# Row sums of w_ada: ScalarE multiplies, GpSimd adds one piece per slab, VectorE takes the last 20 pieces

## What is computed

```python
c_act = jax.nn.silu(c)
mod = c_act @ w_ada[l] + b_ada[l]                  # w_ada: 2048 x 12288
sh1, sc1, gt1, sh2, sc2, gt2 = jnp.split(mod, 6, axis=-1)
h = modulate(rms_norm(x, g_mix[l]), sh1, sc1)
z = h @ w_in[l]                                    # q, k, v of two attentions, index, two gates
# stick-breaking attention, indexed sparse attention, their output products, merge
x = x + gt1[:, None, :] * (merged @ w_out[l])
h = modulate(rms_norm(x, g_ffn[l]), sh2, sc2)
a = causal_dwconv(h @ w_gate[l], conv_w[l], conv_b[l])
y = (jax.nn.silu(a) * (h @ w_up[l])) @ w_down[l]
x = x + gt2[:, None, :] * y
```

## Time and profile before

| | |
|---|---|
| median of 3 runs | 3091.49 us (3090.83 to 3091.84) |
| span of the profiled execution | 3088.4 us |
| PE busy | 2772.0 us (90%) |
| DVE busy | 2006.4 us (65%) |
| ACT busy | 1288.5 us (42%) |
| POOL busy | 1037.5 us (34%) |
| mean granted clock of PE | 0.960 |

### The profile page before, as it was taken

One profiled execution on the slowest core, in us unless ns is written; L12 is line 12 of the kernel. 1 busy time (PEld: TensorE's weight loads), 2 busy tenths in 40 slices (PEclk: granted clock), 3 DMA queues, 4 the chain that ended last, 5 costly groups with the idle time before them and its releaser, 6 DMA issues. The chain is left out here.

```text
span 3088.4 us, 35464 instructions
## 1 busy us (share of the span) xinstructions
PE 2772.0 (90%) x12279; PEld 2258.1 (73%) x12279; DVE 2006.4 (65%) x1808; ACT 1288.5 (42%) x1505; POOL 1037.5 (34%) x538
## 2 busy tenths in 40 slices
PE   0599899989988799999999959998898999999998
PEld 0477787667767678888788748777587888888886
DVE  7776566887975777677766674456655555555554
ACT  1223455334433444444444434444245444444443
POOL 0598454858945433222322250002200111111111
PEclk9989899989999899999999979998999999999999
DMA  9666554746664665655666515454054555555553
GB/s 392 240 205 230 198 206 175 245 144 210 242 234 164 236 204 190 204 195 191 198 204 207 187 55 187 153 177 150 1 164 152 190 190 190 190 191 190 189 190 122
DMA packets 266919, 585.40 MB, mean 190 GB/s; under 512 B 14300, under 2 KB 16676, under 8 KB 263900
## 3 DMA queue, kind: packets, MB, share of 16 engines
q1 hardware_dynamic: 266844, 584.41, 56.1%
HBM read 582.26 MB, written 2.11 MB: 189 GB/s over the span
## 5 line engine op out<-in xcount | busy, mean ns | idle before, releaser
L1206 DVE TENSOR_TENSOR sb_wlo<-sb_raw,sb_whi 128x1024 fp32r<-128x1024 f32 x896 | 1322.9, 1487 | 883.4 <-ACT sb_whi L818 882.5
L818 ACT ACTIVATE sb_whi<-sb_raw 128x1024 fp32r<-128x1024 f32 x896 | 945.2, 1059 | 1452.8 <-PE lin L393 1250.8
L391 PE MATMUL lin<-sb_whi,sb_act_hi 128*128 128x512 f32 x2880 | 1154.9, 401 | 89.7 <-DVE sb_wlo L1206 46.4
L393 PE MATMUL lin<-sb_whi,sb_act_lo 128*128 128x512 f32 x2880 | 1136.2, 395 | 0.0
L392 PE MATMUL lin<-sb_wlo,sb_act_hi 128*128 128x512 f32 x2880 | 1136.0, 394 | 0.0
L391 PEld LDWEIGHTS lin<-sb_whi,sb_act_hi 128*128 128x128 f32 x2880 | 550.7, 191 | 218.9 <-issue 53.2
L393 PEld LDWEIGHTS lin<-sb_whi,sb_act_lo 128*128 128x128 f32 x2880 | 549.6, 191 | 117.9
L392 PEld LDWEIGHTS lin<-sb_wlo,sb_act_hi 128*128 128x128 f32 x2880 | 551.3, 191 | 111.8 <-issue 0.2
L1758 POOL TENSOR_TENSOR sb_ada_in<-sb_ada_in,sb_small 128x1024 f32<-128x1024 f32 x128 | 301.0, 2351 | 293.5 <-DMA sb_ada_in<-in_w_ada_dram 174.7
L1760 POOL TENSOR_TENSOR sb_ada_acc<-sb_ada_acc,sb_ada_in 128x1024 f32<-128x1024 f32 x128 | 383.4, 2995 | 10.0
L391 PE MATMUL lin<-sb_whi,sb_hid_hi 128*128 128x512 f32 x704 | 278.4, 395 | 6.3 <-DVE sb_hid_lo L1487 3.7
(11 more groups left out here) (292 smaller groups left out, 1770.5 us busy)
## 6 DMA issues: line engine op xcount, KB each, us to landing
sb_raw<-in_w_in_dram SPq DMA_DIRECT2D x88, 1024.0 KB, 5.9
sb_raw<-in_ffn_w_gu_dram SPq DMA_DIRECT2D x88, 1024.0 KB, 5.1
sb_ada_in<-in_w_ada_dram SPq DMA_DIRECT2D x128, 512.0 KB, 3.9
sb_raw<-in_gla_w_in_dram SPq DMA_DIRECT2D x48, 1024.0 KB, 5.2
...
```

Of the source, the lines that this page charges most:

```text
L391: pe.matmul(o, x_hi[:, kt + q, t], whi[:, w], start=first and q == 0, stop=False)
L393: m = pe.matmul(o, x_lo[:, kt + q, t], whi[:, w], start=False, stop=last and q == 1)
L818: act.activation(whi[:, idx % RING * HALF:(idx % RING + 1) * HALF], raw[:, idx // 2 % RING, idx % 2 * HALF:(idx % 2 + 1) * HALF], ACT.Copy ...
L1206: dve.tensor_tensor(wlo[:, c], raw[:, idx // 2 % RING, idx % 2 * HALF:(idx % 2 + 1) * HALF], whi[:, c].bitcast(fp32), ALU.subtract).then_i ...
```

## The change

1. **Multiply on ACT, add on POOL.** For chunks 0 to 107 ACT multiplies in place (`ada_scale`), right after it has split the second half of the slab the chunk belongs to. POOL only adds (`ada_add`), and copies instead of adding for the first row block of a piece, so `ada_acc` is no longer cleared. The column copy (`acol`) is gone.
2. **One table places the chunks.** `CHUNKS_AT` gives to each slab, counted from the first of A, its chunks: none for the first four slabs, then one a slab through A, B and to the 12th slab of C1 (chunks 0 to 63), one a slab through C2 and O (64 to 95), four in U's last four slabs, and eight in F1p (one each in slabs 0, 1, 4 and 5, two each in slabs 6 and 7). SP issues the chunk behind its slab; it waits for the addition two chunks earlier (`ada_done`).
3. **The last 20 chunks (108 to 127), two in each round of F1, go to DVE** as one fused multiply and add (`ada_last`), behind the splits of halves 21 and 23.
4. **Moved steps.** `ada_columns(0)` stands after B (on a buffer of its own, `ada_first`), `ada_columns(1)` inside C1 after half 11 of its second round; `gs_ffn` is made after B; the 16 small loads and the wait for `erow`'s write stand behind the first slab of the second round of C1.
5. **Loops A, B, C1, C2, O** are unrolled on SP, ACT and DVE, C1 on PE too. POOL's stages of the attentions keep their order among themselves.

```diff
+ADA_PIECES = (4, 3, 2, 5)
+CHUNKS_AT = {}
+for _n in range(108):
+    _at = 4 + _n if _n < 64 else 8 + _n if _n < 96 else 20 + _n if _n < 102 else (124, 125, 126, 126, 127, 127)[_n - 102]
+    CHUNKS_AT.setdefault(_at, []).append(_n)
...
+    ada_first = at("ada_first", [P, D], XB)
...
         def slab(it, phase, per, s, src):
...
             sp.dma_start(raw[:, s % RING, :].rearrange("p (k n) -> p k n", k=4), src).then_inc(slab_in[s % RING], 16)
+            for n in chunks_after(phase, it, per, s):
+                ada_chunk(n)
-        def ada_chunk(n, piece, j):
+        def ada_chunk(n, kt=None, half=None):
             if not (isinstance(n, int) and n < 2):
-                sp.wait_ge(ada_left, n - 1)
+                sp.wait_ge(ada_done[n % 2 if half is None else half], (n // 2 if half is None else 48 + kt))
...
-        sp.wait_ge(sem("e_out"), 16)
-
-        sp.wait_ge(sem("tt_T"), KT // 2)
-        for h in range(NH):
+        for it in range(4):
+            cols_body(it, "B", 6 * NB)
+
+        def hankels():
+
+            sp.wait_ge(sem("e_out"), 16)
+            sp.wait_ge(sem("ada_T"), 1)
+            for h in range(NH):
...
+        for it in range(2):
+            cols_body(it, "C1", C_GATE, hankels if it else None)
...
         m.then_inc(sem("kix_T"), 1)
-        ada_columns(0)
...
         pe.wait_ge(sem("kix_made"), 1)
-        pe.wait_ge(sem("mod_made"), 1)
...
         pe.wait_ge(sem("sb_out"), NH)
+        ada_columns(0)
...
+                if (it, idx) == (1, 11):
+                    pe.wait_ge(sem("mod_made"), 1)
+                    ada_columns(1)
...
+        def ada_scale(n):
+
+            kt, half = n % 32 // 2, n % 2
+            act.wait_ge(ada_come[half], 8 * (n - half) + 16)
+            act.activation(ada_in[:, half, :], ada_in[:, half, :], ACT.Copy, scale=cact[:, kt:kt + 1]).then_inc(sem("ada_mul"), 1)
+
         def body(it, phase, per, hooks, upto=None, start=RING):
...
                 for step in hooks.get(idx, ()):
                     step()
+                if idx % 2:
+                    for n in chunks_after(phase, it, per, idx // 2):
+                        ada_scale(n)
...
+        def ada_last(it, half):
+
+            c = slice(half * (D // 2), (half + 1) * (D // 2))
+            dve.wait_ge(ada_come[half], 8 * (2 * it + 108) + 16)
+            dve.wait_ge(ada_done[half], 1 * (it + 54))
+            dve.scalar_tensor_tensor(ada_acc[:, c], ada_in[:, half, :], cact[:, ds(6 + it, 1)], ada_acc[:, c], ALU.mult, ALU.add).then_inc(ada_done[half], 1)
...
-        def ada(n, kt, half, col):
+        def ada_add(n, kt=None, half=None):
...
-            pool.wait_ge(ada_come[half], 8 * (n - half) + 16)
-            pool.wait_ge(sem("ada_sum"), n)
-            pool.tensor_tensor(ada_in[:, half, :], ada_in[:, half, :], col.to_broadcast([P, D // 2]), ALU.mult).then_inc(sem("ada_mul"), 1)
             pool.wait_ge(sem("ada_mul"), n + 1)
-            pool.tensor_tensor(ada_acc[:, c], ada_acc[:, c], ada_in[:, half, :], ALU.add).then_inc(sem("ada_sum"), 1)
...
+            if first and n >= 64:
+                pool.wait_ge(sem("ada_T"), n // 32)
+            if first:
+                pool.tensor_copy(acc[:, c], ada_in[:, half, :]).then_inc(ada_done[half], 1)
+            else:
+                pool.wait_ge(ada_done[half], n // 2 if kt is None else 48 + kt)
+                pool.tensor_tensor(acc[:, c], acc[:, c], ada_in[:, half, :], ALU.add).then_inc(ada_done[half], 1)
...
             if g < 3:
-                for k in ((), (0, 1), (2, 3))[g]:
-                    pairs_of(96 + 2 * k, k, 48 + k)
+            for s in ((), (), range(12, 16), range(16, 18))[g]:
+                chunks("U", s)
```

More of the change, by code:

```diff
@@ L265, in _, with cols_body @@
         sp.dma_start(relb[:], A["rel_bias"]).then_inc(sem("rel_in"), 16)
-        def a_body(it):
+        def cols_body(it, phase, col0, after=None):
             for s in range(8):
[L269 to L282, removed]
+                slab(it, phase, 16, s, w_in[:, 4 * (s % 4):4 * (s % 4) + 4, it * 2 * NB + col0 + s // 4 * NB:it * 2 * NB + col0 + s // 4 * NB + NB])
@@ L941, in sb_act @@
             return hooks
-        with act.Fori(0, 3) as it:
+        for it in range(0, 3):
             body(it, "B", 16, drains2(it, "B", lambda k: dsz[:, 0, cols(it, k)], sb_act(it)))
@@ L963, in ix_act @@
             return hooks
-        with act.Fori(0, 2) as it:
+        for it in range(0, 2):
             body(it, "C1", 16, drains2(it, "C1", lambda k: gate_sb[:, 0, cols(it, k)], ix_act(it)))
@@ L1405, in ds_dve @@
             return hooks
-        with dve.Fori(0, 2) as it:
+        for it in range(2):
             body(it, "C2", 16, drains2(it, "C2", lambda k: gate_ds[:, 1, cols(it, k)], ds_dve(it)))
@@ L1546, in hooks @@
                 add(ups, lambda: up(it, phase, 1 if phase != name else 5, ups - AHEAD + 1, j))
+                if n == 0 and phase == name:
+                    for half in range(2):
+                        add(21 + 2 * half, lambda half=half: ada_last(it, half))
                 return hk
@@ L1793, in _ @@
         sb_stage(1, 1)
[L1794 to L1805 removed]
+        for s in range(1, 32):
+            chunks("B", s)
+            h = s // 4 + 2
+            if s % 4 == 3 and h < NH:
+                pool.wait_ge(sem("sb_o"), h - 1)
+                sb_stage(h, h % 2)
+        chunks("C1", 0)
         def ix_stage(p, u):
```

172 lines of the change are left out of this document (69 added, 103 removed).

## The result

| | before | after |
|---|---|---|
| median of the runs | 3091.4 us (3090.83 to 3091.84, 4 runs) | 3008.45 us (3008.22 to 3011.86, 4 runs) |
| span of the profiled execution | 3088.4 us | 3006.7 us |
| mean granted clock of PE | 0.960 | 0.97 |

The ratio is 0.9737, with a 95% interval of 0.9723 to 0.9751: the change saves 83 us of the median, and 81.7 of the profiled span.

The account below looks back on a forecast made before the run. PE was taken to lose time before F1 because POOL and DVE take turns at one shared door. Nine terms summed to -86.5 us from 3088.4, a span of 3001.9, plus 3.1 for the median: 3005 us, range 2970 to 3052.

Parts of the forecast that it names:

- Rival a: Stages B to O: one addition per slab still catches DVE's small steps; 3045 us; chance 0.24 together with rival d.
- the door: Something POOL and DVE share in turns: 1.89 us per POOL chunk operation, 1.22 per DVE subtraction; 12.4 us against PE's 10.9 in A.
- rival d: The moves count, not the multiply, as ACT's multiply holds the door too; near 3047 us; chance 0.24 with Rival a.
- Rival b: All PE waits before F1 go, the far ends of the gains summing to -117; 2974 us; chance 0.12.
- Term 1: A's first round: `features` has the door for itself and the first cast starts sooner; -27 us (-18 to -29).
- terms 8 and 9: F1p: quieter `features` -7 us, two chunks a slab +1.5; F1: fused operations fit DVE's gaps, 0 (0 to +5).
- Term 2: Border from A to B: moved small loads shrink PE's 27.0 us gap to 8; -19 us (-14 to -22).
- An addition alone 1.89 us: POOL's addition of a chunk, undisturbed, taken to cost as much as its undisturbed multiply, 1.89 us; upper bound 2.995.
- Term 3: B's other rounds: the door needs as much as before; -2 us (+8 to -6).
- Rival c: In B to O, ACT waits in order for late chunks, lengthening each head's chain; 3170 us, slower; chance 0.04.
- Terms 4 and 5: C1: less door, but both `ada_columns` at 3.63 us each, -10 us (0 to -14); C2: less contention, -4 (+6 to -12).
- ring turn: Chunk buffers: landing 3.9, multiply 1.06, addition 1.89, one wait 1.22, so 8.1 us, with 10.9 available for two slabs.

Follow-up runs that it names:

- e1: The kernel after, with POOL again making the multiply of chunks 0 to 107 and all moves kept; 3075.78 us, ratio 0.9959.
- e5: The kernel after without POOL's 100 additions of chunks, ACT's multiply freeing the buffer; 2988.35 us, ratio 0.9673.
- e9: e7 with the chunks 96 to 107 placed as in e3; 2977.48 us, ratio 0.9641.
- e2: The kernel before with one move alone, the wait for erow's write and the 16 small loads put behind B; 3080.65 us, ratio 0.9966.
- e7: The kernel after with chunks 0 to 107 done on DVE, one fused multiply and add each; 2989.13 us, ratio 0.9671.
- e4: The kernel after with POOL's staging copy of a head, from the third on, two chunks later in its order; 3005.13 us, ratio 0.9727.
- e6: The kernel after without ACT's multiply, POOL adding the raw chunk once it has landed; 3002.1 us, ratio 0.971.
- e3: The kernel after with chunks 96 to 107 four slabs sooner, one a slab, none in F1p's last two slabs; 2998.26 us, ratio 0.9714.

## Why the prediction was right, and which steps failed

The forecast's mechanism holds: POOL's work beside DVE's made the halves late, and most of the gain (63 of 81.7 us by the spans, with the moves in place) is the multiply that left POOL. Rival a (the door stays busy in the attentions) and rival d (the moves alone) are out; e1 is d made real and gave 3076, not 3047 us. Rival d's own argument, that ACT's multiply in place might hold the door, is out as well: B's subtractions run at 1.21 us in e5 beside ACT's multiplies. Rival b's 2974 us is where e9 lands, but with the additions on DVE.

| term | predicted | measured |
|---|---|---|
| 1 A's first round | -27 | -26.6, and -1.6 in its second |
| 2 A to B | -19 | -19.2 |
| 3 B's other rounds | -2 | +4.0 |
| 4 C1 | -10 | -6.7 |
| 5 C2 | -4 | -11.2 |
| 6 O | -8 | -11.8 |
| 7 U | -11 | -13.7 |
| 8 F1p | -5.5 | +2.1 |
| 9 F1 | 0 | +3.9 in its first round, -0.4 in the others |

Term 1: the cast of `features` is 0.42 us in after (2.56 in the earlier trace rows):

```profile
117.77 0.42 DVE L1265 CAST sb_act_hi<-sb_aff 128x512 fp32r<-128x512 f32 x1
```

and A0 ends at 167.6 us, where 168 was said. Of the signs that the forecast named, this one, the casts and F1's rounds after the first came; the subtraction's mean in C1 is 54.87/33 = 1.66 us, where 1.3 to 1.5 was said, the additions' is 2.65, and SP's waits for chunk buffers still precede a late slab (terms 8 and 9).

Term 2 came within 0.2 us, but not by its parts: the border is 6.4 us long (271.9 to 278.31), where 8 was said, so that it saves 20.6, and the rest of B's first round grew by 1.4. And e2 splits the saving into the loads (10.7 us of B0) and the rest, `ada_columns(0)` above all, whose removal the term did not name.

**Where the price was off.** "An addition alone 1.89 us" was mis-sized, and the trace of before could show it: its shortest addition of 128 took 2.34 us, and the two that DVE's small top-k steps stood beside in C2 took 2.40 and 2.41.

```profile
661.15 2.40 POOL L1760 TENSOR_TENSOR sb_ada_acc<-sb_ada_acc,sb_ada_in 128x1024 f32<-128x1024 f32 x1
```

The shortest of the 100 additions of after took 2.34 us too, and the median is 2.40 us. The Trainium skill (GPSIMD Engine Reference, Elementwise — side-by-side cycle accounting) gives 1.96 for GpSimd's addition against VectorE's; the trace agrees, with 2.40/1.22 = 1.97, and the prediction's estimate of 2.4 us by that ratio was the better number. With it the sum, 3001.9, would lose about 5 us, and the span came 4.8 above it; that this is so close is partly luck, as the terms below show.

Nor does adding up the door give the time of a stage. For A the forecast had 12.4 us of door to 10.9 of PE and called the door the bound; yet A's third round in before ran at PE's pace, with POOL busy for nearly all of it, and PE had no wait from 195 to 302 us:

```profile
257.80:301.30 43.50, 43.50 (x193) 35.70 (x191) 33.36 (x16) 14.65 (x15) 40.81 (x17) 1.00 0.67 217
```

In e1, 6.7 us a slab would make 53.6 us of each round with a chunk on every slab: A's third took 45.7, B's last three 61.8 to 63.5. That POOL's operations lengthen DVE's beside them is shown; how much of it reaches PE depends on the stage, and the sum doesn't say. A smaller slip: ACT's busy share in the stages from A to O is 29% to 58% by the earlier trace rows, and not 24% to 48%; nothing came of it.

**Term 3 had the wrong sign.** Its step was that the door needs as much as before, so the time stays. But the subtraction in B1 to B3 went from 68.50/48 = 1.43 us to 1.92, though in B1 and B2 POOL was busy as long (50.41 us of 105.0, against 51.83 of 98.0). The subtraction in before:

```profile
379.10:532.10 153.00, 68.50 (x48) 0.99 0.55 195
```

After, ACT releases the addition right after the split that releases the subtraction, so the two meet nearly each time; before, POOL ran its two operations on every second slab at its own time. That this is why the same load costs more is argued from the timelines and not isolated by a run. What is shown is that the additions make B's whole loss (e5 and e7: 49.0 a round), and that POOL's copy (e4) or ACT's multiply (e6, 2.6 us less) make little of it. Rival c can be seen in small, at one head, where ACT idled 1.01 us for a chunk (391.93) and then 1.49 us for the slab behind it (394.57); these two runs bound what it costs.

**Terms 4 and 5.** The 3.63 us for `ada_columns` was a price at full clock. In after the first stands behind a stall of 1.69 us and takes 6.99 us, in a window with a granted clock of 0.50. (Between A and B in before it took 6.83, from 320.26 us, so what moved into C1 was no step of 3.63 there either.)

```profile
490.65 6.99 PE L435 MATMUL aux<-sb_con,sb_ada_first 128*128 128x1 f32 x32 [1.69 <-ACT sb_oT_sb L947]
```

```profile
490.60:497.70 7.10, 7.05 (x33) 7.05 (x34) 3.12 (x4) 1.52 (x3) 1.01 (x3) 0.50 0.64 224
```

The 3.4 us above 3.63 are as much as C1 missed its term by (3.3). The stall is tied to the additions: in e5, without them, the same step stands behind 0.83 us and takes 4.51, and C1's first round is 3.2 us shorter. No run isolates the step. In C2 the step "PE waits at the same place anyway: nothing" failed: PE does wait (3.58 us for DVE's drain, in place of 3.63 of `ada_columns` and 0.70 of wait), but the round is 4.8 us shorter, and stays so in e1 where the multiply is undone. 3.0 of it are PE's waits for `qk_ds` in this round, 9.0 us in two places before and 6.0 in one after. Which of the moved steps gives it was not separated; C2's second round gave 6.4, of which e1 keeps 4.3.

**Terms 8 and 9.** The forecast gave two chunks a slab 1.5 us (0 to 4), one ring turn of 8.1 us for each pair; they cost about 10 (e3). The step that failed is the turn. It was counted from issue to landing to ACT at once, but ACT takes a chunk at its place in order, behind the split of its slab. Of POOL's last six chunks, the two that SP issued at 932.32 and 934.62 landed at 936.3 and 940.8; ACT, behind `features` and the splits of F1p, multiplied them at 962.95 and 968.87, and only then could SP issue the next two, with F1p's last slab behind them (SP's rows under e3).

```profile
962.95 1.14 ACT L827 ACTIVATE sb_ada_in<-sb_ada_in,sb_small 128x1024 f32<-128x1024 f32 x1
```

From issue to issue the turns of these two buffers took 34.3 and 37.9 us, and the next two 11.8 and 8.3. With two buffers and two chunks a slab, SP gets to a slab only when ACT is through the second before it (F1p's last slab left at 972.9, when ACT had split the first half of the one before); with one chunk a slab it may be one slab further ahead. In e7 DVE takes the chunks in its order and the same happens (F1's first round 77.2 us). In e6 POOL takes each chunk when it lands, and with the chunks at the same slabs F1's first round is 68.5 us.

In F1p another 2.4 us hang on one small DVE step. It begins inside the second of two additions of POOL and ends, at 936.36 us, with POOL's clear behind them:

```profile
928.97 5.62 POOL L1787 TENSOR_TENSOR sb_ada_acc<-sb_ada_acc,sb_ada_in 128x1024 f32<-128x1024 f32 x2
934.55 1.79 POOL L1910 MEMSET sb_yacc<- 128x2048 f32 x1
```

```profile
933.80 2.56 DVE L1245 TENSOR_SCALAR sb_small<-sb_small 128x2 f32<-128x2 f32 x1 [3.71 <-ACT sb_junk L855]
```

In e9 the same step, with POOL at rest, is

```profile
917.71 0.17 DVE L1259 TENSOR_SCALAR sb_small<-sb_small 128x2 f32<-128x2 f32 x1 [1.19 <-ACT sb_junk L852]
```

The rest of term 9 held: the other nine rounds of F1 are 616.2 us (616.6 before), with two fused operations more on DVE in each. The sum came out near because the misses on both sides largely cancel: terms 3, 4, 8 and 9 came 6.0 + 3.3 + 7.6 + 3.9 = 20.8 us worse than said, terms 5, 6 and 7 and A's second round 7.2 + 3.8 + 2.7 + 1.6 = 15.3 better.
